# Low parts of every fourth weight unit on GpSimd in place of VectorE, in a two-layer hybrid decoder trunk

## What is computed

```
h = RMSNorm(x)
u = h @ w_in[l]                       # (256 x 2048) @ (2048 x 6232)
y = concat[ GLA(u) * silu(g_a) | SSD(u, g_b) | MLA(u) * silu(g_c) | DilatedAttention(u) * silu(g_d) ]
x = x + y @ w_out[l]                  # (256 x 2048) @ (2048 x 2048)
```

## Time and profile before

| | us |
|---|---|
| median of 3 runs | 853.35 (851.84 to 854.38) |
| the profiled execution | 852.73 |
| its span, first to last instruction | 850.9 |
| TensorE busy | 835.6 |
| VectorE busy | 525.7 |
| ScalarE busy | 468.5 |
| GpSimd busy | 62.2 |

### The profile page before, as it was taken

One profiled execution on the slowest core, in us unless ns is written; L12 is line 12 of the kernel. 1 busy time (PEld: TensorE's weight loads), 2 busy tenths in 40 slices (PEclk: granted clock), 3 DMA queues, 4 the chain that ended last, 5 costly groups with the idle time before them and its releaser, 6 DMA issues.

```text
span 850.9 us, 11362 instructions
## 1 busy us (share of the span) xinstructions
PE 835.6 (98%) x4360; PEld 707.7 (83%) x4360; DVE 525.7 (62%) x874; ACT 468.5 (55%) x778; POOL 62.2 (7%) x90
## 2 busy tenths in 40 slices
PE   6999999999999999999999999999999999999998
PEld 5777888998987888888888878889989888888886
DVE  5536874685696656545664478638838965655542
ACT  6555643774855665533556455447557665663331
POOL 1730000000300000000003000001002000000000
PEclk9999999999999999999999999999999999999999
DMA  9895553463655435666548736526535544546663
GB/s 339 299 272 198 196 179 108 114 195 107 183 187 160 142 127 171 184 192 195 184 158 275 245 127 198 174 79 181 163 92 194 181 142 143 170 132 214 199 183 116
DMA packets 46518, 150.99 MB, mean 177 GB/s; under 512 B 5712, under 2 KB 5824, under 8 KB 46208
## 3 DMA queue, kind: packets, MB, share of 16 engines
q1 hardware_dynamic: 43872, 141.71, 52.3%
q0 software_dynamic: 1984, 6.12, 2.7%
q10 hardware_dynamic: 608, 2.43, 0.8%
HBM read 148.13 MB, written 2.11 MB: 177 GB/s over the span
## 4 chain that ended last, share of the span: by engine, by line
PE 88%; DVE 5%; ACT 3%; DMA 2%; issue 1%; SPq 0%; ACTq 0%; DVEq 0%
PE gemm L574 25%; PE gemm L576 25%; PE gemm L575 25%; DMA raw<-in_weights_dram 2%; PE pairs L748 2%; DVE w_lo L1262 2%; PE pairs L644 1%; PE pairs L774 1%; PE pairs L763 1%; DVE u L1385 1%; ACT w_hi L917 1%; PE pairs L598 1%; PE pairs L755 1%; PE pairs L789 1%; DVE o L1361 0%
## 5 line engine op out<-in xcount | busy, mean ns | idle before, releaser
L1262 DVE TENSOR_TENSOR w_lo<-raw,w_hi 128x1024 fp32r<-128x1024 f32 (+1 forms) x287 | 317.9, 1115 | 239.9 <-ACT w_hi L917 239.1
L574 PE MATMUL gemm<-w_hi,a_hi 128*128 128x512 f32 (+1 forms) x1148 | 433.1, 377 | 4.4 <-DVE w_lo L1262 4.4
L576 PE MATMUL gemm<-w_hi,a_lo 128*128 128x512 f32 (+1 forms) x1148 | 422.4, 368 | 0.0
L575 PE MATMUL gemm<-w_lo,a_hi 128*128 128x512 f32 (+1 forms) x1148 | 421.6, 367 | 0.0
L917 ACT ACTIVATE w_hi<-raw 128x1024 fp32r<-128x1024 f32 (+1 forms) x287 | 274.3, 969 | 180.6 <-PE gemm L576 154.7
L574 PEld LDWEIGHTS gemm<-w_hi,a_hi 128*128 128x128 f32 x1148 | 215.8, 188 | 41.6 <-DVE w_lo L1262 6.5
L576 PEld LDWEIGHTS gemm<-w_hi,a_lo 128*128 128x128 f32 x1148 | 215.6, 188 | 35.6
L575 PEld LDWEIGHTS gemm<-w_lo,a_hi 128*128 128x128 f32 x1148 | 216.2, 188 | 33.7 <-issue 1.0
L947 ACT ACTIVATE u<-gemm,st 128x512 f32<-128x512 f32 (+1 forms) x40 | 22.0, 604 | 20.8 <-PE gemm L576 20.8
L491 POOL TENSOR_TENSOR st<-st,powers 128x4 f32<-128x4 f32 (+2 forms) x8 | 2.1, 260 | 419.8 <-ACT arena L1001 221.7
L1118 ACT ACTIVATE arena<-arena,st 128x128 f32<-128x128 f32 (+1 forms) x32 | 13.1, 444 | 28.2 <-DVE st L1488 28.2
(11 more groups left out here) (200 smaller groups left out, 630.8 us busy)
## 6 DMA issues: line engine op xcount, KB each, us to landing
raw<-in_weights_dram SPq DMA_DIRECT2D x223, 512.0 KB, 4.2
raw<-in_weights_dram SPq DMA_DIRECT2D x64, 278.0 KB, 2.8
wuq<-in_mla_w_uq_dram POOLq DMA_DIRECT2D x2, 1152.0 KB, 12.0
x<-in_x_dram SPq DMA_DIRECT2D x4, 512.0 KB, 10.2
o<-ssd_rows ACTq DMA_DIRECT2D x2, 1024.0 KB, 6.2
u<-in_xT_dram SPq DMA_DIRECT2D x3, 512.0 KB, 9.5
out_dram<-x SPq DMA_DIRECT2D x3, 512.0 KB, 6.5
wukv<-in_mla_w_ukv_dram POOLq DMA_DIRECT2D x2, 512.0 KB, 14.3
```

What stands on the lines that cost most here:

```text
L574: pe.matmul(acc_t[t], a_hi[:, k, tok[t]], hi, start=k == 0, stop=False)
L575: pe.matmul(acc_t[t], a_hi[:, k, tok[t]], lo, start=False, stop=False)
L576: last = pe.matmul(acc_t[t], a_lo[:, k, tok[t]], hi, start=False, stop=k == KT - 1)
L1262: TT(w_lo[:, n % SPLIT, 0:c], raw[:, n % RAW, 0:c], w_hi[:, n % SPLIT, 0:c].bitcast(F32), ALU.subtract).then_inc(split_done, 1)
```

## The change

GpSimd makes the low part of each unit n with n % 4 == 3. The counter `split_done` is replaced by two, one for each engine that makes low parts, and `split_of` says which counter and value stand for a unit. The low parts are put into GpSimd's program by a loop over the units that stands behind its setup and the two gate DMAs; the other items of its layer program are tied to values of n in that loop. SyncE's and TensorE's waits go by `split_of`.

```diff
@@ -375,7 +375,8 @@
         row_out, row_in = sem("row_out"), sem("row_in")
         x_turned, x_hi, x_lo = sem("x_turned"), sem("x_hi"), sem("x_lo")
         weights_in = [sem(f"weights_in_{i}") for i in range(RAW)]
-        hi_done, split_done, unit_used = sem("hi_done"), sem("split_done"), sem("unit_used")
+        hi_done, unit_used = sem("hi_done"), sem("unit_used")
+        split = {"dve": sem("split_dve"), "pool": sem("split_pool")}
         stage = {e: sem(f"{e}_stages") for e in ORDER}
         setup = {e: sem(f"{e}_setup") for e in ORDER}
         seen = {e: [] for e in ORDER}
@@ -391,6 +392,15 @@
             return lambda name: (stage[e], l * len(ORDER[e]) + ORDER[e].index(name) + 1)
 
         block = ctx.enter_context(nc.Block())
+
+        def splitter(n):
+
+            return "pool" if n % RAW == RAW - 1 else "dve"
+
+        def split_of(l, n):
+
+            g = l * UNITS + n
+            return (split["pool"], g // RAW + 1) if splitter(n) == "pool" else (split["dve"], g // RAW * (RAW - 1) + g % RAW + 1)
 
         def unit_width(n):
             return BLOCKS[n // UPB][2]
@@ -419,7 +429,8 @@
             for l in range(DEPTH):
                 for n in range(UNITS):
                     w = unit_width(n)
-                    sp.wait_ge(split_done, l * UNITS + n + 1)
+                    if l * UNITS + n >= RAW:
+                        sp.wait_ge(*split_of(l, n - RAW))
                     if (l, n) == (0, 0):
 
                         sp.dma_start(raw[:, 0, WB:2 * WB], weights(l, n)[:, WB:2 * WB]).then_inc(weights_in[0], 16)
@@ -496,19 +507,39 @@
 
                 pool.dma_start(w2[0:GLA_R, :], gla_w2[l]).then_inc(gate_in, 16)
                 pool.dma_start(w2[GLA_R:GLA_R + 1, :], gla_b[l].unsqueeze(0)).then_inc(gate_in, 16)
-                rsqrt("x rs", xrs, xss)
-                for k, src in (("gla_ng", gla_ng), ("ssd_ng", ssd_ng), ("q_ng", q_ng), ("kv_ng", kv_ng), ("q_hg", q_hg),
-                               ("k_hg", k_hg), ("dq_g", dq_g), ("dk_g", dk_g), ("dtb", dt_bias), ("alog", A_log), ("D", D_d)):
-                    pool.dma_start(param[k], src[l].partition_broadcast(P)).then_inc(params_in, 16)
-                pool.dma_start(wuq[:, :, :], w_uq[l].rearrange("(k p) n -> p k n", p=P)).then_inc(params_in, 16)
-                pool.dma_start(wukv[:, :], w_ukv[l]).then_inc(params_in, 16)
-                rsqrt("gla rs", grs, gss)
-                rsqrt("mla crs", crs, css)
-                rsqrt("mla rs 0", mrs[:, 0:8], mss[:, 0:8])
-                rsqrt("mla rs 1", mrs[:, 8:16], mss[:, 8:16])
-                rsqrt("dil rs 0", drs[:, 0:8], dss[:, 0:8])
-                rsqrt("dil rs 1", drs[:, 8:16], dss[:, 8:16])
-                rsqrt("ssd rs", brs, bss)
+                def lo(n):
+
+                    c = UK * unit_width(n)
+                    pool.wait_ge(hi_done, l * UNITS + n + 1)
+                    pool.tensor_tensor(w_lo[:, n % SPLIT, 0:c], raw[:, n % RAW, 0:c], w_hi[:, n % SPLIT, 0:c].bitcast(F32), ALU.subtract).then_inc(split["pool"], 1)
+
+                def parameters():
+                    for k, src in (("gla_ng", gla_ng), ("ssd_ng", ssd_ng), ("q_ng", q_ng), ("kv_ng", kv_ng), ("q_hg", q_hg),
+                                   ("k_hg", k_hg), ("dq_g", dq_g), ("dk_g", dk_g), ("dtb", dt_bias), ("alog", A_log), ("D", D_d)):
+                        pool.dma_start(param[k], src[l].partition_broadcast(P)).then_inc(params_in, 16)
+                    pool.dma_start(wuq[:, :, :], w_uq[l].rearrange("(k p) n -> p k n", p=P)).then_inc(params_in, 16)
+                    pool.dma_start(wukv[:, :], w_ukv[l]).then_inc(params_in, 16)
+
+                for n in range(UNITS):
+                    if splitter(n) == "pool":
+                        lo(n)
+                    if n == 9:
+                        rsqrt("x rs", xrs, xss)
+                        parameters()
+                    if n == 48:
+                        rsqrt("gla rs", grs, gss)
+                    if n == 57:
+                        rsqrt("mla crs", crs, css)
+                    if n == 74:
+                        rsqrt("mla rs 0", mrs[:, 0:8], mss[:, 0:8])
+                    if n == 78:
+                        rsqrt("mla rs 1", mrs[:, 8:16], mss[:, 8:16])
+                    if n == 81:
+                        rsqrt("dil rs 0", drs[:, 0:8], dss[:, 0:8])
+                    if n == 83:
+                        rsqrt("dil rs 1", drs[:, 8:16], dss[:, 8:16])
+                    if n == 94:
+                        rsqrt("ssd rs", brs, bss)
 
                 pool.wait_ge(*reached("dve", l)("yT 3"))
 
@@ -545,7 +576,7 @@
                             pe.wait_ge(x_updated, updated(l - 1, D // WB - 2 + b))
                     first = (l, n) == (0, 0)
                     if not first:
-                        pe.wait_ge(split_done, l * UNITS + n + 1 + RAW)
+                        pe.wait_ge(*split_of(l, n))
                     if U_OUT <= n < U_OUT + UPB and n % 2 == 0:
                         pe.wait_ge(*dve(f"yT {(n - U_OUT) // 2}"))
                     for j in range(UK):
@@ -560,7 +591,7 @@
                             for t in range(T):
                                 pe.matmul(acc_t[t], a_hi[:, k, tok[t]], hi, start=k == 0, stop=False)
                             if j:
-                                pe.wait_ge(split_done, 1 + RAW)
+                                pe.wait_ge(*split_of(0, 0))
                             else:
                                 pe.wait_ge(first_lo, 1)
                             pe.wait_ge(x_lo, j + 1)
@@ -1218,7 +1249,6 @@
 
         @block.vector
         def _(v):
-            v.sem_inc(split_done, RAW)
 
             v.wait_ge(cols_in, 16)
 
@@ -1256,10 +1286,12 @@
                         xT_lo(0, 0)
                         xT_lo(1, 0)
                         v.wait_ge(hi_done, 1)
-                        TT(w_lo[:, 0, WB:c], raw[:, 0, WB:c], w_hi[:, 0, WB:c].bitcast(F32), ALU.subtract).then_inc(split_done, 1)
+                        TT(w_lo[:, 0, WB:c], raw[:, 0, WB:c], w_hi[:, 0, WB:c].bitcast(F32), ALU.subtract).then_inc(split["dve"], 1)
+                        return
+                    if splitter(n) == "pool":
                         return
                     v.wait_ge(hi_done, l * UNITS + n + 1)
-                    TT(w_lo[:, n % SPLIT, 0:c], raw[:, n % RAW, 0:c], w_hi[:, n % SPLIT, 0:c].bitcast(F32), ALU.subtract).then_inc(split_done, 1)
+                    TT(w_lo[:, n % SPLIT, 0:c], raw[:, n % RAW, 0:c], w_hi[:, n % SPLIT, 0:c].bitcast(F32), ALU.subtract).then_inc(split["dve"], 1)
 
                 def yT(j):
```

## The result

| | before | changed |
|---|---|---|
| median, us | 853.48 | 881.19 (879.86 to 882.77) |
| profiled execution, us | 852.73 | 881.22 |
| its span, us | 850.9 | 879.4 |

The account below looks back on a forecast made before the run. TensorE, busy 835.6 of 850.9 us, was taken as the bound, making GpSimd's readiness decisive. The terms 22.2 + 2.0 - 2.2 + 1.6 + 4.2 = +27.8 gave 881 us, range 870 to 890.

Parts of the forecast that it names:

- The reading order: For each moved unit, whether GpSimd's low part is ready between ScalarE's high-part copy and TensorE's first matmul.
- Unit 3, +22.2: Layer 0: GpSimd's setup and gate DMAs precede the first pass, so unit 3 starts at 39.6 instead of 17.44.
- the rival with the short start: Masks land near 20 us and setup operations shorten: unit 3 +15, total 873 or 866; chance 0.10.
- the undisturbed setup: GpSimd's setup before unit 3 runs 5.2 us shorter with VectorE idle, freeing GpSimd at 37.15.
- The price of a pass: One low part on GpSimd takes 2.4 us for a wide unit, 1.4 for a narrow one.
- The 176 us given for all passes: Total GpSimd work for the 72 moved units, 56 wide and 16 narrow: 176 us.
- The clock, +2.0: After TensorE's idle time at unit 3, some ten matmuls run at half rate: +2.0 us, bounds 0 and 2.4.
- What the stop removes, -2.2: Two earlier TensorE waits in the first 47 us, for a late weight load and GpSimd's x scale, vanish: -2.2 us.
- the "about 24" given as a sign to look for: After unit 15, the remaining timeline should be the earlier one moved by a constant of about 24 us.
- Unit 11, +1.6: GpSimd's x scale and 13 parameter DMAs precede unit 11's pass: 0.8 us late in each layer, +1.6 together.
- Tight units, +4.2: Mid-layer units with short budgets: 0.5 at unit 27, 1.0 at 55, 0.6 at other narrow units; +4.2 over both layers.
- The lock: Rival: VectorE and GpSimd holding each other up sets the pace across moved units, about 915 us; chance 0.06.

Follow-up runs that it names:

- the later first unit: Two kernels: against the changed kernel, GpSimd's low parts begin only at unit 15 or unit 7 of layer 0; 859.6 and 872.5 us.
- the wait alone: Kernel before, VectorE making all low parts, but its pass for unit 3 of layer 0 waits until GpSimd's setup is over; 872.33 us.
- the better order: Changed kernel, all 72 passes on GpSimd; layer 0: unit 3's pass before constants, angles after units 11 and 15; both layers: parameter DMAs after unit 19; 856.34 us.
- The experiment with unit 25: Against the 851.26 us kernel (wide-budget passes from unit 23, x scale before angles), unit 25 of both layers also on GpSimd; 852.35 us.
- the later parameters: Changed kernel with the parameter DMAs of both layers behind unit 11's pass instead of ahead of it; 879.47 us.

## Why the prediction was right

**The reading order.** The forecast rested on asking of each moved unit what stands ahead of it on its new engine, not on VectorE's load. The experiments with the later first unit, the wait alone and the better order bear that out, and the relief itself was worth nothing that can be measured (851.87 without it, 851.26 with it). The terms as the traces show them are 22.1 + 2.2 - 2.2 + 1.7 + 4.6 = 28.4, and the traced executions differ by 28.5; that the medians differ by 27.7, within 0.1 of the forecast, is chance at that level.

**Unit 3, +22.2:** measured 22.1 in the timelines, and GpSimd free at 37.16 against 37.15. The hit is luckier than its parts. The tables landed 0.6 us sooner (all that came of the rival with the short start), and the undisturbed setup saved 4.6 us, not 5.2: the three operations of line 480 take 0.85 us alone, where I had taken 0.72 from one that ended behind VectorE's pass, and the one of line 482 takes 0.53, not 0.30. That 0.30 was the row of another form: lines 475, 476 and 484 do two arithmetic steps in one instruction, lines 480 and 482 one, and the form with two is the shorter here at the same size, 0.30 against 0.53 at 128 columns and 0.40 against 0.85 at 256 (why is open). The price of a pass was right (2.35; mean of the wide ones 2.48, of the narrow ones 1.42, for 2.4 and 1.4). The 176 us given for all passes was a slip: 56 by 2.4 and 16 by 1.4 are 157, and 161.7 were measured; nothing hung on it.

**The clock, +2.0:** measured 2.2. Taking the row of the start as the model, against the clock column's 1.00 there, was right: the granted clock is 0.56 behind the stop, which agrees with the rule of the Trainium skill, TensorE: Matmul & The Clock Gate, Part 1, that the forecast had weighed.

**What the stop removes, -2.2:** 1.05 at unit 6 and 1.13 at unit 13, in the changed kernel and in both kernels in which VectorE waits at unit 3 for 8 us or more. Behind unit 14 the lag is 22.8 us, as the terms say; the "about 24" given as a sign to look for did not follow from them.

**Unit 11, +1.6:** 0.80 and 0.88; taken out by itself, 1.7 less. In layer 0 the pass of GpSimd behind its DMAs:

```profile
61.87 2.39 POOL L514 TENSOR_TENSOR w_lo<-raw,w_hi 128x1024 fp32r<-128x1024 f32 x1
62.16 3.20 DVE L1294 TENSOR_TENSOR w_lo<-raw,w_hi 128x1024 fp32r<-128x1024 f32 x1 [1.49 <-ACT w_hi L948]
...
64.32 0.50 PE L605 MATMUL gemm<-w_hi,a_hi 128*128 128x512 f32 x1 [0.63 <-POOL w_lo L514]
```

**Tight units, +4.2:** measured 4.6, the sum right and its split not. Units 27 cost 0.27 each (0.5 forecast), units 55 1.17 each (1.0), the other narrow units 0.15 in all (1.2). In their place came 1.5 us in layer 1, which the sum did not have: slow matmuls behind the wait at unit 55. So the units' own part is 3.0 us, and that the total still fits is luck.

**The lock.** As a rival (about 915 us) it was wrong; as a price it is real. Before, 56 wide passes at 1.226 and 16 narrow at 0.731 us were 80 us of VectorE. The durations of all its instructions add up to only 33 us less, so its other work took 47 us longer (its remaining wide passes 1.31 us in place of 1.23, the convolution's operations 0.545 in place of 0.476); its busy time, in which overlaps count once, fell by 28. All the operations that got longer have two inputs in SBUF; those with at most one did not (a low part of the activations, with one input in PSUM, 1.223 and 1.225 us; line 1413, 1445 in the changed kernel, 0.346 in both). TensorE's own work covers nearly all of the longer operations. The experiment with unit 25 shows the place where it doesn't, and there my theory forecast a gain of 0.8 us that turned into a loss: it counted GpSimd's time against the budget, and not VectorE's chain beside it.

## What to carry to other kernels

Before work is moved to an idle engine, read that engine's queue at the moment of each first use: of a one-time setup, DMA issues or a wait in front of it, all that lasts beyond the moment at which the work is due is paid in full (unit 3 was 19.1 us late from the setup alone), and being idle on average says nothing. If TensorE is 98% busy, relieving another engine can win at most the waits that TensorE has for it (4.4 us here), and only if the new place is sooner for those very units. And work moved from VectorE to GpSimd doesn't leave VectorE free: 80 us of passes taken away made its busy time 28 us shorter.

## What the runs showed of the hardware

**A short wait can halve TensorE's rate afterwards.** In ten passages of unit 55 in five kernels (the changed one, both with later first units, the mended order, the later parameters) TensorE waited for some 2 us for GpSimd; in five of them matmuls behind it came at 0.23 us instead of 0.13, for some 3.4 us, and cost 1.5 us more. (In two of the five the first six still came at 0.13.) The granted clock is 0.51 from 617.4 to 620.9 us in the first of the two kernels below, and 1.00 from 592.6 to 596.0 in the second. Layer 1 of the changed kernel, and of the kernel in the mended order, where it did not happen:

```profile
617.38 0.54 PE L605 MATMUL gemm<-w_hi,a_hi 128*128 128x278 f32 x1 [1.92 <-POOL w_lo L514]
617.71 0.43 PE L606 MATMUL gemm<-w_lo,a_hi 128*128 128x278 f32 x1
617.94 0.43 PE L607 MATMUL gemm<-w_hi,a_lo 128*128 128x278 f32 x1
...
621.05 0.29 PE L606 MATMUL gemm<-w_lo,a_hi 128*128 128x278 f32 x1
621.19 0.29 PE L607 MATMUL gemm<-w_hi,a_lo 128*128 128x278 f32 x1
```

```profile
592.67 0.40 PE L616 MATMUL gemm<-w_hi,a_hi 128*128 128x278 f32 x1 [1.93 <-POOL w_lo L520]
592.91 0.29 PE L617 MATMUL gemm<-w_lo,a_hi 128*128 128x278 f32 x1
593.04 0.29 PE L618 MATMUL gemm<-w_hi,a_lo 128*128 128x278 f32 x1
```

The waits are the same, 1.92 and 1.93 us. The two groups of times of the mended order, some 3 us apart with a lower mean clock in the upper one, fit zero against two such passages; only one of its six executions has a trace, so that is argued and not shown. What decides between the two outcomes of a wait of 2 us is not shown. Waits of 8, 13, 19 and 23 us at the start lowered the rate each time.

**The clock column says nothing at the very start.** It shows 1.00 while the first ten matmuls go at half rate, and 0.50 to 0.56 for the same spacing behind a later stop. In the trace of the kernel before, the first reading of the clock stands at 11.6 us, when these matmuls are over (9.9 to 12.8 us in the others): the 1.00 ahead of it is no measurement, and the spacing is.
